# A hybrid decoder layer on one core: the end of each attention head interleaved with the next head's first projection

## The reference: what is computed

```python
x_lru, z_lru, q, k, v, z_gla, a_lo, gate_logits = jnp.split(proj, IN_SPLITS, axis=-1)
# branch A: causal conv (width 4) -> RG-LRU recurrence -> * silu(z_lru) -> w_lru_o
# branch B, 4 heads, DK 128, DV 256: gated linear attention in chunks
g = log_sigmoid(a_lo @ w_a2 + b_a) / 16
att = einsum('btd,bsd,btsd->bts', q, k, exp(b_t - b_s));  o = att @ v + (q * exp(b)) @ S
S_new = exp(b_last) * S + (k * exp(b_last - b)).T @ v
o = o * rsqrt(mean(o * o) + EPS) * gla_norm_g;  y_b = (o * silu(z_gla)) @ w_gla_o
# merge
out = x + (sigmoid(gA) * y_a + sigmoid(gB) * y_b) @ w_out;  then a last RMSNorm
```

## Time and profile before

| | us |
|---|---|
| median of 3 runs | 1174.18 (1167.6 to 1174.44) |
| the profiled execution | 1172.13 |
| its span in the trace | 1170.4 |
| PE busy | 1142.9 (98%) |
| DVE, ACT, POOL busy | 543.3, 424.1, 207.2 |
| mean granted TensorE clock | 0.991 |

### The profile page before, as it was taken

One profiled execution on the slowest core, in us unless ns is written; L12 is line 12 of the kernel. 1 busy time (PEld: TensorE's weight loads), 2 busy tenths in 40 slices (PEclk: granted clock), 3 DMA queues, 4 the chain that ended last, 5 costly groups with the idle time before them and its releaser, 6 DMA issues.

```text
span 1170.4 us, 17706 instructions
## 1 busy us (share of the span) xinstructions
PE 1142.9 (98%) x6872; PEld 1104.5 (94%) x6872; DVE 543.3 (46%) x718; ACT 424.1 (36%) x560; POOL 207.2 (18%) x128
## 2 busy tenths in 40 slices
PE   5999999989999999999999999999999999999997
PEld 4999999989999999999999999999989999999886
DVE  5677777885000001763484357437635001434433
ACT  6444455555111112543542453345435121111321
POOL 2541111212121211110112011111102111210000
PEclk9999999999999999999999899999999999999999
DMA  6121111111212122110311121021102103342332
GB/s 212 45 63 52 46 40 40 40 36 56 73 55 73 61 86 78 46 31 19 114 36 36 42 90 36 18 86 46 35 18 77 54 18 111 119 156 82 99 108 72
DMA packets 95632, 76.17 MB, mean 65 GB/s; under 512 B 3944, under 2 KB 88808, under 8 KB 95608
## 3 DMA queue, kind: packets, MB, share of 16 engines
q1 hardware_dynamic: 84512, 61.42, 17.6%
q10 hardware_dynamic: 11096, 14.44, 3.6%
HBM read 62.04 MB, written 13.80 MB: 65 GB/s over the span
## 4 chain that ended last, share of the span: by engine, by line
PE 96%; ACT 1%; DVE 1%; issue 1%; ACTq 0%; POOL 0%; DVEq 0%; POOLq 0%
PE ps L470 28%; PE ps L472 28%; PE ps L471 28%; PE ps L618 2%; PE ps L681 1%; PE ps L660 1%; PE ps L652 1%; PE ps L662 1%; PE ps L645 1%; PE ps L700 1%; PE ps L497 1%; PE ps L589 1%; PE ps L609 1%; PE ps L693 0%; DVE xt L1244 0%
## 5 line engine op out<-in xcount | busy, mean ns | idle before, releaser
L470 PE MATMUL ps<-xn,whi 128*128 128x364 f32 (+1 forms) x1344 | 452.3, 337 | 2.7 <-ACT tr L939 2.5
L472 PE MATMUL ps<-xn,wlo 128*128 128x364 f32 (+1 forms) x1344 | 442.8, 329 | 0.0
L471 PE MATMUL ps<-xn,whi 128*128 128x364 f32 (+1 forms) x1344 | 442.5, 329 | 0.0
L430 POOL TENSOR_TENSOR wlo<-raw,whi 128x1024 fp32r<-128x1024 f32 x72 | 186.4, 2589 | 843.3 <-ACT whi L857 843.3
L470 PEld LDWEIGHTS ps<-xn,whi 128*128 128x128 f32 x1344 | 254.7, 190 | 6.3 <-ACT tr L939 2.8
L471 PEld LDWEIGHTS ps<-xn,whi 128*128 128x128 f32 x1344 | 254.9, 190 | 0.2
L472 PEld LDWEIGHTS ps<-xn,wlo 128*128 128x128 f32 x1344 | 254.2, 189 | 0.0
L857 ACT ACTIVATE whi<-raw 128x1024 fp32r<-128x1024 f32 x72 | 75.8, 1053 | 151.6 <-PE ps L472 87.1
L471 PE MATMUL ps<-act_s,whi 128*128 128x364 f32 (+1 forms) x384 | 125.9, 328 | 0.0
L472 PE MATMUL ps<-act_s,wlo 128*128 128x364 f32 (+1 forms) x384 | 125.9, 328 | 0.0
L470 PE MATMUL ps<-act_s,whi 128*128 128x364 f32 (+1 forms) x384 | 125.8, 328 | 0.0
(11 more groups left out here) (249 smaller groups left out, 1372.5 us busy)
## 6 DMA issues: line engine op xcount, KB each, us to landing
raw<-in_w_in SPq DMA_DIRECT2D x56, 512.0 KB, 3.8
branch_a<-keep ACTq DMA_DIRECT2D x8, 546.0 KB, 2.8
mal<-branch_a SPq DMA_DIRECT2D x8, 544.0 KB, 4.6
xt<-in_x_prompt SPq DMA_DIRECT2D x8, 512.0 KB, 7.2
raw<-in_w_lru_o SPq DMA_DIRECT2D x8, 512.0 KB, 3.6
st<-in_state_gla ACTq DMA_DIRECT2D x4, 1024.0 KB, 5.4
out<-st ACTq DMA_DIRECT2D x4, 1024.0 KB, 4.7
raw<-in_w_gla_o SPq DMA_DIRECT2D x8, 512.0 KB, 5.5
```

The lines of the kernel that those rows point to most:

```text
L430: pool.tensor_tensor(wlo[:, c % 2], raw[:, c % 2], whi[:, c % 2].bitcast(F32), ALU.subtract).then_inc(s["lo_ok"], 1)
L470: pe.matmul(dst, wh, mh, start=first, stop=False)
L471: pe.matmul(dst, wh, ml, start=False, stop=False)
L472: return pe.matmul(dst, wl, mh, start=False, stop=last)
```

## The change

1. **PE**: job 0 of the first head goes ahead of the loop. In the loop the head starts with job 1; the next head's job 0 (`part(6, bankA, ...)`; for the last head, the merge gate's first job) is spread over the end of the head: one step after every second sequence of Os, then steps between nrm0 to nrm2, which now precede the outer products, and steps between sKV0 to sKV3. Job 5 is finished ahead of the outputs.
2. **ACT**: the z gate's tanh on job 5 goes ahead of the copies of O; `whi` for the next head's job 1 goes between the squares; w_a2 is split at the end of the head before; the logarithms wait for the second `sq_sum`, and write to `inv` (the second half of `qk`), not `kt`; k's copy waits for og1_ok; the load of `st0` and `whi` of job 3 move behind level_exp(1).
3. **SP** loads `w_a2`, behind the head's first weight.
4. **DVE**: the z gate's product first, both sums of squares, two of four outer products, the first output half normed and gated (og0_ok), the other two products, the second half (og1_ok).
5. **After the heads**: ACT evacuates the merge gate's first bank after 3 of the 8 copies of the gated output, the second after all. DVE, no longer ACT, waits for the state stores. The last head is written out a second time in ACT's and DVE's programs.

```diff
     steps += [(f"O{g}{d}", "act") for g in range(2) for d in range(VH)] + [("Os", "act")]
+    steps += [(f"nrm{j}", "act") for j in range(PIECES)]
     steps += [(f"sKV{n}", "dve") for n in range(NSEQ // 2)]
-    steps += [(f"nrm{j}", "act") for j in range(PIECES)]
...
+        inv = qk[:, 1, :]
...
                     load(6 * h + (N_GLA + j), (N_GLA + j) % 2, w_in[:, :, bass.ds(h * step + col, P)])
+                    if j == 0:
+                        sp.wait_ge(s["wa2_lo"], h + ONE)
+                        sp.sem_inc(s["sp_passed"], 1)
+                        for r in range(6):
+                            sp.dma_start(wa2_raw[r * RANK:(r + 1) * RANK, :], t["w_a2"][0][:, bass.ds(h * P, P)]).then_inc(s["wa2_in"], 16)
...
+            pe.wait_ge(s["lo_ok"], N_GLA + 1)
+            piece(N_GLA, bankA, xn, 0)
+            piece(N_GLA, bankA, xn, 1)
+            pe.wait_ge(s["alo_ok"], PIECES)
+            piece(N_GLA, bankA, xn, 2).then_inc(s["job_done"], 1)
+            pe.wait_ge(s["tails_ok"], 2)
+            pe.wait_ge(s["ma_ok"], KT + ONE)
             with pe.Fori(0, HEADS) as h:
...
-                    between = iter(range(2, KT - 1))
+                    between = iter(range(KT))
...
-                            if q in (2, 5) or (q == NSEQ - 1 and d == 0):
+                            if q % 2 == 1 and (d == 0 or q < NSEQ - 1):
                                 k = next(between)
-                                part(5, bankB, 2, range(k, k + 1))
+                                part(6, bankA, 0, range(k, k + 1))
...
-                start_job(0)
+                pe.wait_ge(s["wa2_lo"], h + (ONE + 1))
+                start_job(1)
                 pe.wait_ge(s["zg_silu"], 2 * h + ONE)
-                part(0, bankA, 0)
-                part(0, bankA, 1)
-                pe.wait_ge(s["alo_ok"], PIECES)
-                part(0, bankA, 2)
-                pe.wait_ge(s["tails_ok"], 2)
-                pe.wait_ge(s["wa2_lo"], h + (ONE + 1))
+                part(1, bankB, 0, EARLY)
                 gate(0)
                 gate(1)
-                start_job(1)
-                pe.wait_ge(s["ma_ok"], KT + ONE)
-                part(1, bankB, 0)
+                part(1, bankB, 0, LATE)
                 gate(2)
                 part(1, bankB, 1)
                 part(1, bankB, 2)
...
-                part(5, bankB, 2, range(2))
+                part(5, bankB, 2)
...
+                start_job(6)
+                pe.wait_ge(s["zg_silu"], 2 * h + (ONE + 1))
                 pe.wait_ge(s["st0_in"], 16 * (h + 1))
                 c_step("Os", sample_output)
+                part(6, bankA, 0, range(KT - 1, KT))
+                pe.wait_ge(s["sq_sum"], 2 * h + 1)
+                mean_square(0)
+                part(6, bankA, 1, range(0, 2))
+                mean_square(1)
+                part(6, bankA, 1, range(2, 4))
+                pe.wait_ge(s["sq_sum"], 2 * (h + 1))
+                mean_square(2)
+                part(6, bankA, 1, range(4, KT))
                 pe.wait_ge(s["ktm_ok"], h + 1)
                 sample_outer(0)
+                part(6, bankA, 2, range(0, 1))
                 sample_outer(1)
-                part(5, bankB, 2, range(KT - 1, KT))
+                part(6, bankA, 2, range(1, 3))
                 sample_outer(2)
+                part(6, bankA, 2, range(3, 5))
                 sample_outer(3)
-                pe.wait_ge(s["sq_sum"], 2 * (h + 1))
-                for j in range(PIECES):
-                    mean_square(j)
+                part(6, bankA, 2, range(5, KT))
 
 
             pe.wait_ge(s["zg_silu"], 2 * HEADS + ONE)
-            with pe.Fori(0, KT // 2) as i:
+            job(0, N_GB + 1, bankB, xn)
+            with pe.Fori(1, KT // 2) as i:
...
+            def wa2_high(h):
+                act.wait_ge(s["wa2_in"], 96 * h + 96)
+                act.activation(wa2[:, :], wa2_raw[:, :], ACT.Copy).then_inc(s["wa2_hi"], 1)
+
+            def act_head(h, last):
...
+                act.wait_ge(s["og0_ok"], h + ONE)
                 for j in range(PIECES):
                     full(f"g{j}")
                     act.sem_inc(s["act_passed"], 1)
...
+                act.wait_ge(s["og1_ok"], h + ONE)
                 act.activation(p3(kb[:, :]), slot3(bankB), ACT.Copy).then_inc(s["k_ok"], 1)
-                hi(3 * h, N_GLA + 3)
                 level_exp(0)
                 level_exp(1)
+                hi(3 * h, N_GLA + 3)
+                act.wait_ge(s["st0_out"], 16 * h + ONE)
+                act.dma_start(st0[:, :, :], t["state_gla"][0].rearrange("b h p v -> h p b v")[h]).then_inc(s["st0_in"], 16)
...
+                job_at(5)
+                act.wait_ge(s["zg_silu"], 2 * h + (ONE + 1))
+                act.activation(p3(vT[:, :]), slot3(bankB), ACT.Tanh, scale=0.5).then_inc(s["zg_tanh"], 1)
...
                 act.wait_ge(*emptied(h, "O11"))
                 squares(slice(0, SEQ))
+                hi(3 * h, N_GLA + 7)
...
-                job_at(5)
-                act.wait_ge(s["zg_silu"], 2 * h + (ONE + 1))
-                act.activation(p3(vT[:, :]), slot3(bankB), ACT.Tanh, scale=0.5).then_inc(s["zg_tanh"], 1)
-
+                if not last:
+                    wa2_high(h + 1)
+                act.wait_ge(s["sq_sum"], 2 * h + 2)
...
-                    act.activation(kt[:, j * PIECE:(j + 1) * PIECE], ps[:, bank(f"nrm{j}"), 0:PIECE], ACT.Ln,
+                    act.activation(inv[:, j * PIECE:(j + 1) * PIECE], ps[:, bank(f"nrm{j}"), 0:PIECE], ACT.Ln,
                                    bias=ssum[:, 31:32]).then_inc(s["c_act"], 1)
...
-                hi(3 * h, N_GLA + 7)
                 act.wait_ge(*emptied(h, "nrm2"))
-                act.activation(kt[:, :], kt[:, :], ACT.Exp, scale=-0.5).then_inc(s["n_rstd"], 1)
+                act.activation(inv[:, :], inv[:, :], ACT.Exp, scale=-0.5).then_inc(s["n_rstd"], 1)
...
-            act.wait_ge(s["og_ok"], 2 * HEADS + ONE)
-            act.wait_ge(s["st_out"], 16 * HEADS + ONE)
-            act.wait_ge(s["st0_out"], 16 * HEADS + ONE)
-            with act.Fori(0, KT) as i:
+            wa2_high(0)
+            with act.Fori(0, HEADS - 1) as h:
+                act_head(h, False)
+            act_head(HEADS - 1, True)
+
...
+            act.wait_ge(s["og0_ok"], HEADS + ONE)
+            act.wait_ge(s["og1_ok"], HEADS + ONE)
+
+            def gated_hi(i):
                 act.activation(act_s[:, 0, i, :], keep[:, i, :], ACT.Copy).then_inc(s["act_hi"], 1)
-            with act.Fori(0, KT // 2) as i:
-                for j, b in ((0, bankA), (1, bankB)):
-                    act.wait_ge(s["act_lo"], 2 * i + (KT + j + 1))
-                    act.wait_ge(s["job_done"], 2 * i + (N_GB + j + 1))
-                    act.activation(p3(keep[:, 2 * i + j, :]), slot3(b), ACT.Tanh, scale=0.5,
-                                   bias=dvec[:, 2 * i + j, V_BMB:V_BMB + 1]).then_inc(gb_tanh[j], 1)
-                    hi(i, N_GB + j + 2)
+
+            def gate_b(i, j):
+                act.wait_ge(s["act_lo"], 2 * i + (KT + j + 1))
+                act.wait_ge(s["job_done"], 2 * i + (N_GB + j + 1))
+                act.activation(p3(keep[:, 2 * i + j, :]), slot3((bankA, bankB)[j]), ACT.Tanh, scale=0.5,
+                               bias=dvec[:, 2 * i + j, V_BMB:V_BMB + 1]).then_inc(gb_tanh[j], 1)
+                hi(i, N_GB + j + 2)
...
+            for i in range(3):
+                gated_hi(i)
+            gate_b(0, 0)
+            with act.Fori(3, KT) as i:
+                gated_hi(i)
+            gate_b(0, 1)
+            with act.Fori(1, KT // 2) as i:
+                gate_b(i, 0)
+                gate_b(i, 1)
...
+            def dve_head(h, last):
...
+                dve.wait_ge(s["zg_tanh"], 2 * h + 2)
+                dve.scalar_tensor_tensor(p3(keep[:, 2 * h + 1, :]), p3(vT[:, :]), 1.0, slot3(bankB), ALU.add, ALU.mult).then_inc(s["zg_silu"], 1)
                 add_squares(0)
-                for n in range(NSEQ // 2):
-                    if n == 2:
-                        add_squares(1)
+                add_squares(1)
...
-                dve.wait_ge(s["zg_tanh"], 2 * h + 2)
-                dve.scalar_tensor_tensor(p3(keep[:, 2 * h + 1, :]), p3(vT[:, :]), 1.0, slot3(bankB), ALU.add, ALU.mult).then_inc(s["zg_silu"], 1)
...
+                def gated_output(d):
+                    dve.scalar_tensor_tensor(oo[d][:, :], oo[d][:, :], vec[:, 2 * h + d, R_GN:R_GN + 1], inv[:, :], ALU.mult, ALU.mult).then_inc(s["o_norm"], 1)
+                    dve.wait_ge(s["o_norm"], 2 * h + (d + 1))
+                    dve.tensor_tensor(keep[:, 2 * h + d, :], keep[:, 2 * h + d, :], oo[d][:, :], ALU.mult).then_inc(s[f"og{d}_ok"], 1)
+
+                add_outer(0)
+                add_outer(1)
+                if not last:
+                    wa2_low(h + 1)
                 dve.wait_ge(s["n_rstd"], h + 1)
-                for d in range(VH):
```

(41 more changed lines are left out.)

6 lines of the change are left out of this document (removed).

## The result

| us | before | after |
|---|---|---|
| median, on one chip | 1169.08 (1164.98 to 1175.1, 10 runs) | 1161.62 (1159.4 to 1165.01, 10 runs) |
| the profiled execution | 1172.13 | 1159.4 |
| its span | 1170.4 | 1157.7 |
| mean granted clock | 0.991 | 0.994 |

A forecast was written before the change was run, and what follows sets the result against it. PE, busy 98% of the span, was taken as the bound. From the profiled execution, 1172.1 - 6.6 (clock) - 1.6 (joints) + 0.3 (handover) + 1.6 (after the last head) = 1165.8 us; range 1161 to 1172.5.

The forecast's parts named there:

- The clock, -6.6 us: Heads' ends: thin work in Os lets the clock fall in three heads; denser steps remove all three falls, -6.6 us.
- PE's own joints, -1.6 us: Heads' ends: bank waits shrink against three more joints between unlike matmuls; about -0.4 a head, -1.6 us for four.
- The handover, +0.3 us: From a head's end to the next head's gate matmuls: PE waits 0.1 us at g2 at each of three boundaries.
- its end of -4.0: Far end of the joints term over four heads: all bank waits go and the joints are free.
- The lower end that I gave, -1.0 a head: Far end of the joints term for one head: all bank waits go and the joints are free.
- The rival in which the norm sets the pace: Next head's g0 waits for DVE's norm; 5 us later means PE stands 4 us at three boundaries: 1187.4 us, chance 0.08.
- After the last head, +1.6 us: Merge gate's third job: its `wlo` hangs on a longer chain, so PE waits 1.2 to 2.1 us.
- a wait for POOL of none: Sign set beforehand: no PE wait for `wlo` at the third merge gate job would prove the +1.6 us term wrong.
- J: Time at a head's end when job 0 is done, put at 13.2 us after the end of Os.
- More is gained than I count: Heads' ends and merge gate: bank waits go fully (-4.0) and the third merge weight is in time: 1161.5 us, chance 0.20.

The follow-up runs named there:

- e4: The changed kernel run once more without a change, as the level for others on its chip: 1161.24 us, ratio 0.9899 to the kernel before.
- e11: The changed kernel run a third time without a change, as a level on its chip: 1159.98 us, ratio 0.992 to the kernel before.
- e1: The changed kernel with the old mixture in Os, 5 steps among the 16 sequences and the other 3 behind: 1166.55 us, ratio 0.9948.
- e2: The changed kernel with no step in Os and all eight behind it: 1170.22 us, ratio 0.9986.
- e3: The kernel before with only 7 steps of job 5 in Os, one after every second sequence, in place of 5: 1167.9 us, ratio 0.997.
- e6: The changed kernel with the four outer products in a row and their 8 steps behind them: 1164.76 us, ratio 0.9948.
- e5: The changed kernel with the three mean squares in a row behind both sums of squares, the 8 steps after them: 1168.66 us, ratio 0.9984.
- e7: The changed kernel with DVE's old order, all four outer products and then both halves of the norm: 1162.02 us, ratio 0.9923.
- e8: The changed kernel with the merge gate's first two banks evacuated only after all 8 copies of the gated output: 1170.26 us, ratio 0.9987.
- e9: The changed kernel with two steps of job 5 moved ahead of the z gate's turn and three `whi` copies put later or earlier: 1157.4 us.
- e10: The changed kernel with one `whi` moved behind branch A's last product instead of ahead of it: 1161.0 us, ratio 0.992.

## Why the prediction was right or wrong

**The clock, -6.6 us: right in place and cause.** In after, e4 and e11 the heads' ends run at full clock, e1 and e2 bring the falls back. In the profiled pair the term is the 6.6 us, on the chip of e3 and e4 about 6. In the comparison with 1169.08 it can be only some 3 (1169.1 less the 1166 that e3 leaves), as executions of before differ in how many falls they hold, and the prediction had one of them.

**PE's own joints, -1.6 us: the term that was mis-sized.** This is the step of the prediction that failed. With the handover it made -1.3; measured are -5.5, of them -3.9 over the three distances from head to head. As the handover cost 1.2 of that, the joints and bank waits by themselves gained some 6.7 us, four times the term and beyond its end of -4.0. Two prices were wrong. A mean square between steps was put at 0.75 us, near the 0.79 in a row. I gave that price to the work, though the row itself names a wait for a bank; it costs 0.61. An outer product was put at 0.6 without waits; it costs 0.475, and 0.2 of the old 0.68 a product ((876.46 - 873.25 - 0.50) / 4) were time in front of it and behind its first matmul, under the size that the list of waits shows. I take them for short bank waits: in e6 the two products that wait show the same longer first distance, 0.22 us, where the two that don't have 0.12. Small work at a head's end takes 8.5 us beside its steps, where the old kernel took 9.9: -1.4 a head instead of -0.4, measured in the last head, whose wait ahead of the mean squares was the shortest of the four. e5 and e6 take the steps away from between the small pieces and lose 1.5 and 1.1 us at each head's end. Together that is more than the 1.4, as their order is not the old kernel's either; so they show where the time lay, and not its size. The lower end that I gave, -1.0 a head, was not low enough.

**The handover, +0.3 us: the mechanism was right, the size too small.** PE waits 0.4 us at g2 by the list and 1.2 us by distance (0.50, 0.48 and 0.18), and never at g0. The prediction had 0 to 0.6 at each boundary and took 0.1. The chain behind it, after the first head, answers to the earlier trace rows; DVE, then ACT:

```profile
560.78 1.84 DVE L1585 SCALAR_TENSOR_TENSOR st<-st,dlast,ps 128x256 f32<-128x256 f32 x4 [5.86 <-PE ps L707]
562.65 0.28 DVE L1442 TENSOR_TENSOR wa<-wa_raw,wa 32x128 fp32r<-32x128 f32 x1
562.96 1.36 DVE L1590 SCALAR_TENSOR_TENSOR gb<-gb,vec,qk 128x1092 f32<-128x1092 f32 x1
...
565.57 1.65 DVE L1585 SCALAR_TENSOR_TENSOR st<-st,dlast,ps 128x256 f32<-128x256 f32 x4
```

```profile
568.14 1.08 ACT L1079 ACTIVATE qb<-ps 128x1092 f32<-128x1092 f32 x1 [6.85 <-DVE st L1585]
...
570.07 1.01 ACT L1085 ACTIVATE gb<-ps,vec 128x364 f32<-128x364 f32 x2
```

DVE goes through the list without a pause: 0.28 us for w_a2, where 0.3 was estimated. The rival in which the norm sets the pace is refuted twice over: the exponential ends at 561.3, ahead of DVE's need, and even the old order (e7) costs nothing between heads.

**After the last head, +1.6 us: the chain was right, but the wait is not there.** The chain in after, by ACT, DVE and POOL, and PE's start of the third merge job:

```profile
881.49 3.13 ACT L1186 ACTIVATE act_s<-keep 128x1092 fp32r<-128x1092 f32 x3 [8.18 <-DVE keep L1592]
...
885.11 1.18 ACT L1191 ACTIVATE keep<-ps,dvec 128x1092 f32<-128x1092 f32 x1 [0.49 <-DVE act_s L1411]
886.18 1.05 ACT L876 ACTIVATE whi<-raw 128x1024 fp32r<-128x1024 f32 x1
```

```profile
883.78 3.71 DVE L1411 TENSOR_TENSOR act_s<-keep,act_s  x3 [2.38 <-ACT act_s L1186]
```

```profile
887.31 2.46 POOL L436 TENSOR_TENSOR wlo<-raw,whi 128x1024 fp32r<-128x1024 f32 x1 [23.37 <-ACT whi L876]
```

```profile
889.88 0.37 PE L476 MATMUL ps<-xn,whi 128*128 128x364 f32 x1
```

The order of the steps is the one forecast, with DVE waiting for the store (issued at 878.83, landed 4.4 us later; the row names ACT, whose first copy had been done for over a microsecond). But POOL is done at 889.77, and PE starts the job at 889.88, in its regular rhythm: 11.92 us behind the second one. e4 and e11 have no wait there either. By the prediction's own sign (a wait for POOL of none) this term is wrong. Counted from J, here 877.96, the subtraction ended at J + 11.8 and not at 13.2 to 14.1. It began at J + 9.4 instead of 9.9 to 10.8: the store landed at J + 5.3, where I had 6.3 at the earliest, and my sum held some 0.3 us that it does not name (7.5 + 1.16 + 1.05 is 9.7, and with the 3.14 it is 12.9). And it took 2.46 us instead of the 3.14 of the earlier trace rows, as DVE was idle from 887.49 to 888.48. In before POOL had begun at 898.72, while DVE was at its last low part until 899.61. I carried over a duration that held a collision into a place without it. e8 shows what the early evacuation is worth: without it the new order would have cost all of its gain. In the kernel before it wasn't needed, as the first merge job still lay ahead of PE.

The three terms behind the clock were forecast at +0.3 us together; measured are -5.5. Another 0.8 came from how the profiled execution started, and 0.3 went the other way in the second projection. That is the 6.4 us between the forecast and the profiled 1159.4; against the median of 1161.62 it is 4.2. "More is gained than I count" (0.20) was the case that came in kind: the bank waits went and the third merge weight was in time. That its 1161.5 us is so near the median of 1161.62 is luck, as it counts 4.0 us of waits from 1172.1, where the pair has 5.5 and the median before is 3 us lower.

## What to carry to other kernels

Where PE is busy and its clock still falls, look for thin matmuls in a row and count how many dense ones stand between: here the number of falls in four heads followed it, 0 with seven steps, 3 with five, 4 with none. Price small work by the distance between starts in a place with no wait: durations "in a row" through a ring of two banks hold waits of 0.1 to 0.6 us that a table of waits shows only in part, and dense work put between takes them away. When a reordering uses up the cover of a chain (here the first merge job), the part of the change that shortens that chain can be worth as much as the whole gain (e8: 8.2 us); a plan that moves work forward must bring it along.

## What was not expected

A stretch at full clock can end later than one at half. Behind branch A, after ran at 0.50 from 250.0 to 253.4, and e4 at 1.00; e4 reached its first `act_s` job ready to go and then stood for 2.6 us. DVE's last product there, in after and in e4, and POOL's subtraction in both:

```profile
263.26 1.30 DVE L1383 TENSOR_TENSOR keep<-hh,tz 128x1092 f32<-128x1092 f32 x1
```

```profile
264.08 3.30 DVE L1383 TENSOR_TENSOR keep<-hh,tz 128x1092 f32<-128x1092 f32 x1
```

```profile
263.92 2.91 POOL L436 TENSOR_TENSOR wlo<-raw,whi 128x1024 fp32r<-128x1024 f32 x1 [14.94 <-ACT whi L876]
```

```profile
263.18 3.05 POOL L436 TENSOR_TENSOR wlo<-raw,whi 128x1024 fp32r<-128x1024 f32 x1 [13.38 <-ACT whi L876]
```

```profile
276.47 0.40 PE L476 MATMUL ps<-act_s,whi 128*128 128x364 f32 x1 [2.60 <-DVE act_s L1411]
```

In after DVE's product starts first (263.26, POOL 263.92) and takes 1.30 us. What is caught there is a small copy behind it, for which PE does not wait; it takes 2.32 us, where e4 has 0.16:

```profile
264.54 2.32 DVE L1385 COPY tails<-hh 128x8 f32<-128x8 f32 x1
```

In e4 PE's faster jobs let ACT's `whi` through earlier, POOL starts first (263.18, DVE 264.08), and the product takes 3.30. From the last of branch A's gate matmuls (the start of its last record) to that job it is 29.53 us in e4 and 28.32 in after: the full clock saves 1.4 us, and the wait of 2.6 takes them back, and more. All five traces at full clock there with that order (e4, e5, e6, e8, e9) have 3.30 to 3.32 us for the product, and the seven at half clock have 1.30. The Trainium skill, "SBUF — State Buffer" (Terms, shared port pair), has DVE and GpSimd lock a common port pair, the loser blocked for the whole instruction; the rows agree with it. In e4 POOL is done at 266.23 and the product 1.15 us later; in after POOL is done at 266.83 and the small copy at 266.86. e10 took this collision away (1.30 at full clock, and 28.28 us for the same distance), but POOL's subtraction then met the first low part (2.36 us instead of 1.30), and PE still waited 1.4 us, for ACT (`keep`, L1012).
